# First RMS norm summed by TensorE before the first weight unit, unit 1 on the normalised input, and unit 14 instead of units 13 and 15 at full float32

## What is computed

```python
def rms_norm(x, g):
    y = x * lax.rsqrt(jnp.mean(x * x, axis=-1, keepdims=True) + EPS)
    return y * g

# layer 0
h = rms_norm(x, norm_g)
a, bv, bg, z = jnp.split(h @ w_in, [A_W, A_W + B_W, A_W + 2 * B_W], axis=-1)
ya = grouped_linear(multiscale_pool(a), pool_w) * pool_scale     # windows 2, 4, 8, 16
u = bv * sigmoid(bg)
u = depthwise_causal_conv(u, conv_w, 31 taps) + conv_b
yb = silu(layer_norm(u))
x = x + concat(ya, yb) * silu(z) @ w_out
# layer 1
q, k, v, z = jnp.split(rms_norm(x, g1) @ w_in1, 4, axis=-1)
x = x + (attention(rms(q), rms(k), v, ALiBi, causal) * silu(z)) @ w_out1
```

## Time and profile before

| | |
|---|---|
| median of 3 runs | 343.16 us (343.01 to 343.24) |
| the profiled execution's own time | 343.25 us |
| its span, first to last instruction | 341.4 us |
| TensorE busy | 331.6 us (97%) |
| VectorE busy | 264.9 us (78%) |
| ScalarE busy | 217.0 us (64%) |
| granted TensorE clock, mean of the span | 0.997 |
| weight loads | 49 of 1 MB |

### The profile page before, as it was taken

How to read it: one execution, slowest core, us unless ns; L and a number is a source line. 1 busy time by engine, 2 the same in 40 slices (tenths; PEclk the granted TensorE clock), 3 DMA queues, 4 the chain that set the end, 5 groups by cost and what they waited for, 6 DMA issues and landing times.

```text
span 341.4 us, 5640 instructions
## 1 busy us (share of the span) xinstructions
PE 331.6 (97%) x2164; PEld 297.9 (87%) x2164; DVE 264.9 (78%) x491; ACT 217.0 (64%) x415; POOL 34.3 (10%) x46
## 2 busy tenths in 40 slices
PE   7999999999999999999999999999999999998994
PEld 7899999998989999989999999988877666787884
DVE  3998988999989999989885799648535777767433
ACT  5756776959799991045774457835757576675520
POOL 0000011223242200000000000004400312200000
PEclk9999999999999999999999999999999999999998
DMA  7986037898999866232609433781463333000003
GB/s 277 392 346 265 6 131 179 269 248 199 286 221 247 270 161 265 117 125 98 274 10 418 188 125 128 257 354 60 188 246 123 125 124 123 2 1 2 0 2 124
DMA packets 11115, 59.54 MB, mean 174 GB/s; under 512 B 1232, under 2 KB 1360, under 8 KB 4816
## 3 DMA queue, kind: packets, MB, share of 16 engines
q1 hardware_dynamic: 8064, 53.78, 42.5%
q0 software_dynamic: 2880, 5.24, 8.7%
q10 hardware_dynamic: 144, 0.15, 0.2%
HBM read 52.88 MB, written 1.05 MB: 158 GB/s over the span
## 4 chain that ended last, share of the span: by engine, by line
PE 61%; DVE 23%; ACT 8%; DMA 3%; issue 3%; SPq 0%; ACTq 0%; DVEq 0%
PE bank L974 15%; PE bank L976 15%; PE bank L975 15%; DVE w_lo L646 8%; PE bank L1032 6%; DVE scratch L759 4%; PE bank L1006 4%; DVE scratch L764 4%; DMA raw<-w 3%; PE bank L1190 2%; ACT scratch L469 2%; PE bank L1200 2%; ACT w_hi L392 1%; ACT side_ring L446 1%; DVE scratch L730 1%
## 5 line engine op out<-in xcount | busy, mean ns | idle before, releaser
L646 DVE TENSOR_TENSOR w_lo<-raw,w_hi 128x1024 fp32r<-128x1024 f32 x76 | 89.2, 1220 | 12.2 <-ACT w_hi L392 12.0
L392 ACT CAST w_hi<-raw 128x1024 fp32r<-128x1024 f32 x76 | 75.2, 1047 | 6.4 <-PE bank L976 4.6
L974 PE MATMUL bank<-h_hi,w_hi 128*128 128x256 f32 x208 | 59.6, 287 | 0.6 <-DVE w_lo L646 0.6
L976 PE MATMUL bank<-h_hi,w_lo 128*128 128x256 f32 x208 | 58.8, 283 | 0.0
L975 PE MATMUL bank<-h_lo,w_hi 128*128 128x256 f32 x208 | 58.8, 283 | 0.0
L1006 PE MATMUL bank<-H,raw 128*128 128x256 f32 x256 | 56.8, 379 | 1.6 <-DMA raw<-w 1.6
L1006 PEld LDWEIGHTS bank<-H,raw 128*128 128x128 f32 x256 | 48.0, 190 | 8.1 <-DMA raw<-w 1.8
L759 DVE SCALAR_TENSOR_TENSOR scratch<-scratch,params 128x256 f32<-128x256 f32 x114 | 47.0, 480 | 4.4 <-ACT scratch L482 4.3
L974 PE MATMUL bank<-ya_hi,w_hi 128*128 128x256 f32 x144 | 42.7, 297 | 0.0
L974 PEld LDWEIGHTS bank<-h_hi,w_hi 128*128 128x128 f32 x208 | 39.9, 192 | 1.8 <-issue 1.7
L975 PE MATMUL bank<-ya_lo,w_hi 128*128 128x256 f32 x144 | 40.7, 282 | 0.0
(11 more groups left out here) (99 smaller groups left out, 528.8 us busy)
## 6 DMA issues: line engine op xcount, KB each, us to landing
raw<-w SPq DMA_DIRECT2D x49, 1024.0 KB, 5.4
side_v<-side_ring POOLq DMA_DIRECT2D x20, 256.0 KB, 6.3
X<-xT SPq DMA_DIRECT2D x2, 512.0 KB, 5.2
out<-X SPq DMA_DIRECT2D x4, 256.0 KB, 2.7
consts<-const SPq DMA_DIRECT2D x1, 290.0 KB, 13.5
params<-vec ACTq DMA_DIRECT2D x1, 149.0 KB, 5.0
```

What stands on the lines that cost most here:

```text
L392: nc.scalar.copy(halves(w_hi, cut_slot(n), half), halves(raw, n % RAW, half)).then_inc(hi_cut, 1)
L646: nc.vector.tensor_tensor(halves(w_lo, cut_slot(n), half), halves(raw, n % RAW, half), halves(w_hi, cut_slot(n), half).bitcast(F32), ALU.s ...
L974: nc.tensor.matmul(dst, wh, ah, start=start, stop=False, skip_group_check=True)
L976: return nc.tensor.matmul(dst, wl, ah, start=False, stop=stop, skip_group_check=True)
```

## The change

TensorE runs 15 small matmuls in place of 20. Then it adds up the squares itself: eight matmuls against ones, one for each tile of squares, in pairs that wait for ScalarE's squares, ahead of unit 0. VectorE's first fold is gone. Unit 0 still works on the weighted input, now in a tile of its own (`H0`), and its output is still scaled afterwards. Unit 1 now works on the normalised and split H like all later units: the first split of the unnormalised input (four `high_h`, four `low_h`) and the late scaling of unit 1 are gone, and normalising, splitting H and cutting unit 1 are interleaved on both engines. `NATIVE` has 14 in place of 13 and 15, so there is one more split unit. The ring of cut slots is shifted so that it meets layer 1's slots as before. The planner reads `NATIVE`, so its hand-out of the taps changes with it, which the diff does not show: the planner's functions, worked through with both sets, give these numbers of VectorE's instructions (products, singles) for each step, with steps 2 to 10 alike:

| step | 11 | 12 | 13 | 14 | 15 | 16 | 17 | 18 | 19 | 20 | 21 |
|---|---|---|---|---|---|---|---|---|---|---|---|
| before | 5, 2 | 0, 0 | 3, 6 | 2, 4 | 5, 6 | 0, 8 | 0, 8 | 0, 6 | 0, 10 | 0, 12 | 0, 0 |
| after | 2, 0 | 2, 0 | 1, 4 | 3, 4 | 4, 6 | 0, 8 | 0, 8 | 0, 6 | 0, 10 | 0, 12 | 0, 10 |

```diff
--- before.py
+++ after.py
@@ -53,8 +53,8 @@
 O1 = [45 + i for i in range(4)]
 NU = 49
 
-NATIVE = frozenset((0, 5, 7, 9, 11, 13, 15, 17, 21, 22, 25))
-WARM = 20
+NATIVE = frozenset((0, 5, 7, 9, 11, 14, 17, 21, 22, 25))
+WARM = 15
 RAW = 4
 CUT = 4
 
@@ -90,7 +90,7 @@
 
 def cut_slot(n):
 
-    return cut_index(n) % 3 if n < Z1[0] else (n - Z1[0]) % 4
+    return (cut_index(n) - cut_index(Z1[0])) % 3 if n < Z1[0] else (n - Z1[0]) % 4
 
 
 def released(n):
@@ -209,7 +209,7 @@
 CONV_PLAN, TILE_DONE, PRODUCT_USED = conv_plan()
 
 
-EARLY = (BG[0], BV[0]), (Z1[0], Z1[1])
+EARLY = (BG[0],), (Z1[0], Z1[1])
 
 
 def hybrid_trunk(nc, xT, w, vec, const, out):
@@ -266,6 +266,7 @@
         FX = part(2 * 15).rearrange("p (c t) -> p c t", c=2)
         assert at <= 12654
         PR = SZ[:, 0:KD, :]
+        H0 = SZ[:, KD:2 * KD, :]
         SQ = YP
         at = 0
         SZ1 = part(KD * S).rearrange("p (c t) -> p c t", c=KD)
@@ -381,14 +382,14 @@
 
         @block.scalar
         def _(act):
-            def cut_hi(n):
+            def cut_hi(n, parts=(0, 1)):
 
                 if n >= NU or n in NATIVE:
                     return
                 act.wait_ge(raw_in[n % RAW], 16 * (n // RAW + 1))
                 if slot_free(n):
                     act.wait_ge(unit_done, slot_free(n))
-                for half in range(2):
+                for half in parts:
                     nc.scalar.copy(halves(w_hi, cut_slot(n), half), halves(raw, n % RAW, half)).then_inc(hi_cut, 1)
 
             def square(group, m, source):
@@ -409,13 +410,13 @@
 
             def high_h(step, m):
 
-                act.wait_ge(h_ready, 4 * step + m + 1)
-                to = h_hi if step % 2 else ya_hi
+                act.wait_ge(h_ready, 4 * (step + 1) + m + 1)
+                to = ya_hi if step % 2 else h_hi
                 nc.scalar.copy(to[:, 2 * m:2 * m + 2, :], H[:, 2 * m:2 * m + 2, :]).then_inc(hhi_ready, 1)
 
             def late_gate(layer, i, dst, func, done):
 
-                act.wait_ge(late, 2 * layer + i + 1)
+                act.wait_ge(late, layer + i + 1)
                 nc.scalar.activation(dst, dst, func).then_inc(done, 1)
 
             act.dma_start(V_[:, :], vec).then_inc(vec_in, 16)
@@ -425,14 +426,15 @@
                 if m % 2 == 0:
                     act.wait_ge(x_in[m // 2], 16)
                 square(0, m, X)
-            for m in range(4):
-                high_h(0, m)
-            cut_hi(1)
             take_root(bank[4], 1)
             prime(ACT.Sigmoid)
+            cut_hi(1, (0,))
+            high_h(0, 0)
+            high_h(0, 1)
+            cut_hi(1, (1,))
+            high_h(0, 2)
+            high_h(0, 3)
             cut_hi(2)
-            for m in range(4):
-                high_h(1, m)
             cut_hi(CUTS[2])
             late_gate(0, 0, SG[:, :], ACT.Sigmoid, sig_ready)
 
...
@@ -649,13 +651,13 @@
             def gained(layer, m):
 
                 for c in (2 * m, 2 * m + 1):
-                    last = nc.vector.tensor_scalar(H[:, c, :], X[:, c, :], column((G0, G1)[layer] + c), None, ALU.mult)
+                    last = nc.vector.tensor_scalar((H0, H)[layer][:, c, :], X[:, c, :], column((G0, G1)[layer] + c), None, ALU.mult)
                 last.then_inc(h_ready, 1)
 
             def low_h(step, m):
 
                 dve.wait_ge(hhi_ready, 4 * step + m + 1)
-                hi, lo = (h_hi, h_lo) if step % 2 else (ya_hi, ya_lo)
+                hi, lo = (ya_hi, ya_lo) if step % 2 else (h_hi, h_lo)
                 nc.vector.tensor_tensor(lo[:, 2 * m:2 * m + 2, :], H[:, 2 * m:2 * m + 2, :],
                                         hi[:, 2 * m:2 * m + 2, :].bitcast(F32), ALU.subtract).then_inc(hlo_ready, 1)
 
@@ -681,17 +683,18 @@
                 nc.vector.reciprocal(rinv[:, :], root[:, :]).then_inc(rinv_ready, 1)
                 dve.wait_ge(rinv_ready, n)
 
-            def over_rms(layer):
-
-                if layer == 0:
-                    dve.wait_ge(unit_done, BG[0] + 1)
+            def normed_h(layer, m):
+
+                nc.vector.tensor_tensor(H[:, 2 * m:2 * m + 2, :], (H0, H)[layer][:, 2 * m:2 * m + 2, :],
+                                        rinv[:, :].unsqueeze(1).to_broadcast([P, 2, S]), ALU.mult).then_inc(h_ready, 1)
+
+            def over_rms():
+
                 for m in range(5):
                     if m < 4:
-                        nc.vector.tensor_tensor(H[:, 2 * m:2 * m + 2, :], H[:, 2 * m:2 * m + 2, :],
-                                                rinv[:, :].unsqueeze(1).to_broadcast([P, 2, S]),
-                                                ALU.mult).then_inc(h_ready, 1)
+                        normed_h(1, m)
                     if m:
-                        low_h(2 * layer + 1, m - 1)
+                        low_h(2, m - 1)
 
             def scale_late(layer, i, dst):
 
@@ -706,13 +709,18 @@
                 if m % 2 == 0:
                     dve.wait_ge(x_in[m // 2], 16)
                 gained(0, m)
-            fold(0, 4)
-            for m in range(4):
-                low_h(0, m)
-            cut_lo(1)
             take_inverse(1)
+            normed_h(0, 0)
+            normed_h(0, 1)
+            cut_lo(1, (0,))
+            normed_h(0, 2)
+            low_h(0, 0)
+            low_h(0, 1)
+            normed_h(0, 3)
+            low_h(0, 2)
+            cut_lo(1, (1,))
+            low_h(0, 3)
             cut_lo(2)
-            over_rms(0)
             scale_late(0, 0, SG2)
 
             def window_sums(g):
@@ -783,10 +791,6 @@
                     dve.wait_ge(sig_ready, i + 1)
                     dve.wait_ge(unit_done, m + 1)
                     value = bank[m % 4][:, :].rearrange("p (c t) -> p c t", c=2)
-                    if m in EARLY[0]:
-                        scale_late(0, 1, W1[:, :, 0:S])
-                        dve.wait_ge(late, 2)
-                        value = W1[:, :, 0:S]
                     nc.vector.tensor_tensor(U[:, 2 * i:2 * i + 2, PAD:PAD + S], value, SG2, ALU.mult).then_inc(u_ready, 1)
                 if m in A:
                     window_sums(m - A[0])
...
@@ -991,7 +995,7 @@
 
                 if k % 4 == 0:
                     arrived(n, k // 4)
-                if h_wait == 0 and n in NATIVE:
+                if n == 0:
                     if k % 2 == 0:
                         pe.wait_ge(h_ready, k // 2 + 1)
                 elif h_wait is not None and k % 2 == 0:
@@ -1003,7 +1007,7 @@
                     dst = bank[n % 4][:, c * S:c * S + S]
                     start, stop = k == 0 and c == 0, k == KD - 1
                     if n in NATIVE:
-                        last = nc.tensor.matmul(dst, wr, H[:, k, :], start=start, stop=stop, skip_group_check=True)
+                        last = nc.tensor.matmul(dst, wr, (H if n else H0)[:, k, :], start=start, stop=stop, skip_group_check=True)
                     else:
                         last = product(dst, wp, (hi[:, k, :], lo[:, k, :]), start, stop)
                 if k == KD - 1:
@@ -1043,14 +1047,15 @@
 
                 if folds:
                     pe.wait_ge(folded, folds)
-                else:
-                    pe.wait_ge(sq_ready, 12)
                 for c in tiles:
+                    if not folds and c % 2 == 0:
+                        pe.wait_ge(sq_ready, 8 + c // 2 + 1 if dst is bank[0] else c // 2 + 1)
                     summed = nc.tensor.matmul(dst[:, 0:S], ones[:, :], SQ[:, c, :], start=(c == 0),
                                               stop=(last and c == tiles[-1]), skip_group_check=True)
                 if last:
                     summed.then_inc(rms_sum, 1)
 
+            square_sums(0, range(KD), bank[4], True)
             for n in range(PW):
                 if n >= 4:
                     m = n - 4
@@ -1063,9 +1068,7 @@
                     elif m in A:
                         pe.wait_ge(a_ready, m - A[0] + 1)
                 for k in range(KD):
-                    channel_step(n, k, {0: 0, 1: 0, 2: 1}.get(n))
-                    if n == 0 and k == 3:
-                        square_sums(3, (0,), bank[4], True)
+                    channel_step(n, k, 0 if n == 1 else None)
 
 
             n = PW
...
@@ -1152,9 +1155,9 @@
                 if n % 4 == 0:
                     pe.wait_ge(root_ready, 3)
                 for k in range(KD):
-                    channel_step(n, k, {Z1[0]: 2, Z1[2]: 3}.get(n))
+                    channel_step(n, k, {Z1[0]: 1, Z1[2]: 2}.get(n))
                     if n == Z1[0] and k == 1:
-                        square_sums(8, (0, 1), bank[0], False)
+                        square_sums(5, (0, 1), bank[0], False)
                     if n == Z1[0] and k == 2:
                         square_sums(0, (6, 7), bank[0], True)
```

More of the change, by code:

```diff
@@ L533, in _ @@
                 square(2, m, X)
-                high_h(2, m)
+                high_h(1, m)
             cut_hi(Z1[1])
@@ L538, in _ @@
             for m in range(4):
-                high_h(3, m)
+                high_h(2, m)
```

(6 more changed lines are left out.)

## The result

The change made the kernel slower: 348.51 us (median of 4 runs, 348.24 to 348.97) against 343.13 us (343.01 to 343.24), a ratio of 1.0158 with a 95% interval of 1.0142 to 1.0174. The forecast was 343.7 us, with a range of 341.3 to 345.2.

A forecast was written before the change was run, and what follows sets the result against it. TensorE, busy 97%, was taken as the bound, but its 2.5 us gain is given back in one 2.8 us wait for VectorE's taps before the mean: 343.25 + 0.5 = 343.75 us, 343.7 as a median, range 341.3 to 345.2.

The forecast's parts named there:

- What bounds the kernel: Whole kernel: TensorE, 97% busy, sets the pace, but VectorE's last taps have only 2.1 us in hand at the channel mean.
- The tail (+5.16 us): VectorE, steps 16 to 21: ten singles moved into step 21 (+3.96 us), behind a gating product and low part (+1.2 us).
- lead: How far VectorE runs ahead of the kernel before: 2.45 us when the taps begin, 2.65 us after step 15.
- TensorE's start (+0.1): Warming, eight sums and unit 0 on TensorE: sums from 6.5 to 9.95, unit 0 ending at 16.86, +0.1 us in all.
- the second rival: VectorE's lead is smaller, lost in the interleaved start or a late cut 13: 344.9 us with lead 1.5; chance 0.27.
- Steps 11 to 15 (lead +0.2): VectorE there: -1.1 us of work, -0.9 of idle time, +1.8 of waits, sum -0.2 us, making the lead 2.65.
- The two waits that stand on POOL's queue keep their places: The side chain's two waits were forecast not to move, and the weight loads to cost nothing.
- The third rival: TensorE's clock falls in the wait before the mean: 2.1 us on top of 0.5, giving 345.9 us; chance 0.05.
- The wait forecast, 2.8 us: TensorE, at the channel mean from 145.9, waits 2.8 us for VectorE's tap of tile 0, which ends at 148.7.
- the 0.5 us that were summed: The channel mean begins at 148.8 against 148.30, and this +0.5 us reaches the kernel's end.

The follow-up runs named there:

- the planner as before: The changed kernel with the planner still counting units as before (13 and 15 native, 14 split), giving two short TensorE waits at unit 16: 342.80 us, ratio 0.9985.
- the units alone: The kernel before with unit 14 native, 13 and 15 split, and the ring of cut slots moved, without the new start: 349.44 us, ratio 1.0181.

## Why the prediction was wrong

*What bounds the kernel.* This reading held: the matter was VectorE's last taps against the mean, and TensorE gave back what it gained there in one wait. TensorE stood before the mean at 151.07 - 4.20 = 146.87; 145.9 was forecast, and 0.6 to 0.8 of the difference is the late start (below; unit 1 began at 17.46, forecast 16.86).

*The tail (+5.16 us)* held: from 149.03 with a lead of 0.38 it gives 153.8, and 153.70 was measured.

*TensorE's start (+0.1)* was mis-sized. The step said that the clock's rise lies before 6.5 us because it does in the trace of before, and it summed by that one row. Here 30 records took 6.46 us where I had reckoned on some 5.6, and the sums began at 7.28, not at 6.5. That is +0.8 on the root, and it is why the lead was 1.69 and not 2.45. The sign that I had named for the second rival, a sigmoid after 29, was met (29.35); but the interleaved start that this rival blamed took the time that I had given it (from the reciprocal at 11.45 to step 1 at 23.20, forecast 10.6 to 22.4), and only its late beginning was missed. Over these executions the warming's fifteen matmuls took 5.14 to 6.46 us, a spread of 1.3 us. The rule of the Trainium skill that I had set beside the row (TensorE: Matmul & The Clock Gate, Part 1: the moment of the rise drifts from run to run, by half a microsecond to either side) was the better guide in kind, and too small in size: the prediction made 0.25 us of it.

*Steps 11 to 15 (lead +0.2)*: the wait for cut 13 was forecast at 1.1 and measured at 1.05; without the side chain the lead would have stayed at 1.7, so 0.2 was too much.

*"The two waits that stand on POOL's queue keep their places"* failed: a cost of zero without a look at what shares the DMA engines. Unit 14 being native and 15 split, load 18 waits for unit 14's end and load 19 for cut 15, and both fall at about 104, ahead of the side transfer at 104.7. Before, load 19 waited for unit 15's end, near 111. The pair of transfers then took 10.0 and 12.7 us, where its counterpart before, at 106.1 and 106.9, took 4.7 and 5.2; ScalarE waited 2.71 us and VectorE 1.30. Holding back load 19 brought the pair to 6.8 and 8.6 us and removed both waits. That the two loads alone make the pair slow is not shown: with the planner as before they went out together too, and a pair that followed 2.5 us behind load 19 was quick. The mean's start: 0.5 + 0.75 + 0.2 + 1.3 = 2.75, and 2.77 was measured.

*The clock in the wait.* The third rival named it, priced at 2.1 us and given 0.05. It was the largest single term, 3.25 us. The step that failed is the use of the nearest row: a gap of 1.62 us without a fall was taken as evidence for one of 2.8. In the profiled executions the clock stayed up in waits of 0 to 1.76 us before the mean, and fell in all four of 2.95 to 4.20 us (mean 5.2 to 6.7 us long); the other executions of these four kernels, which were not profiled, show the same low mean clock of 0.990 to 0.995. Filling the wait kept the clock. The Trainium skill (TensorE: Matmul & The Clock Gate, Part 1) says that an idle TensorE is throttled back to 1.2 GHz. The granted clock of 0.50 behind the wait of 4.20 us agrees. The wait forecast, 2.8 us, was already next to the shortest one in which it fell, so a chance of 0.05 was not borne out by any row. The sum took a wait of 2.8 us at its own length and put nothing for the clock behind it; the mean at half clock cost 3.25 us.

With the start's 0.75, the 0.2 of steps 11 to 15, the side chain's 1.3 and the clock's 3.25 on the 0.5 us that were summed, the mean ends 6.0 us late.

## What to carry to other kernels

Price a long idle stretch of TensorE (here 2.95 us and more) twice: its length, and the work behind it at half clock. The version with two short waits (1.8 us in sum) was 5.7 us faster than the one with a single wait of 4.20 us. When a unit changes its kind, look at which loads its release lets go and at what else is on the DMA engines then. And where a planner hands out work by a cost table, read its last step: what doesn't fit is put there, ahead of the engine that waits.

## What was not expected of the hardware

The start of full clock is not a fixed point of a program: the same fifteen matmuls took 5.14 us in one execution and 6.37 in another, and all that follows moved by 1.0 us (the mean at 146.62 and 147.63). A fallen clock is not one price either: the eight matmuls of the mean, whose record behind a wait is 3.69 us long at full clock, took 5.22 to 5.29 us after waits of 2.95 to 3.43 us and 6.70 us after one of 4.20. One kernel can pay either: the units alone took 347.52 us at a mean granted clock of 0.995 and 348.85 to 350.16 us at 0.990. And the kernel before is not wholly free of it: of 57 executions beside the experiments, three took 344.43 to 346.06 us at 0.993 to 0.994, the others showing 0.996 or more. None of the three was profiled, so where the clock fell in them is open.
